# Rounded two-pass scores over stacked key halves, keys and queries single-buffered and projected last, latents' weights in one tile

## The reference, cut to what matters

```python
def fox_attend(q, k, v, cum_q, cum_k, pos_q, pos_k):
    s = jnp.einsum('bqhd,bkhd->bhqk', q, k).astype(jnp.float32) * (HEAD_DIM ** -0.5)
    decay = jnp.transpose(cum_q, (0, 2, 1))[..., :, None] - jnp.transpose(cum_k, (0, 2, 1))[..., None, :]
    visible = pos_k[None, :] <= pos_q[:, None]
    p = jax.nn.softmax(jnp.where(visible, s + decay, NEG_INF), axis=-1)
    return jnp.einsum('bhqk,bkhd->bqhd', p.astype(v.dtype), v)

def sb_attend(q, k, v, pos_q, pos_k):
    z = jnp.einsum('bqhd,bkhd->bhqk', q, k).astype(jnp.float32) * (HEAD_DIM ** -0.5)
    before = pos_k[None, :] < pos_q[:, None]
    log_beta = jnp.where(before, jax.nn.log_sigmoid(z), NEG_INF)
    log_rest = jnp.where(before, jax.nn.log_sigmoid(-z), 0.0)
    later = lax.cumsum(log_rest, axis=log_rest.ndim - 1, reverse=True) - log_rest
    a = jnp.exp(log_beta + later)
    return jnp.einsum('bhqk,bkhd->bqhd', a.astype(v.dtype), v)

# layer 1, mla_project
    z = h @ w_down                       # D_MODEL x (384 + 256 + 32)
    cq, ckv, kr = jnp.split(z, [Q_LORA, Q_LORA + KV_LORA], axis=-1)
```

## Time and profile before

| | before |
|---|---|
| median of 3 runs | 1449.56 us |
| profiled execution | 1455.13 us, span 1453.4 us |
| busy share PE / PEld / DVE / ACT / POOL | 83% / 57% / 45% / 27% / 17% |
| mean granted TensorE clock | 0.919 of full |
| first layer's eight pairs | 45.05 to 341.2 us of the span |
| latents of layer 1 | 722 to 791 us |

### The profile page before, as it was taken

The page is one execution under the profiler, slowest core; times in us unless marked ns, Lnnn a source line. Parts: engine busy times, 40 slices in busy tenths (PEclk is TensorE's granted clock), DMA queues, the critical chain, the costliest instruction groups (busy, mean ns, idle before and its releaser), DMA issues. The chain is left out here.

```text
span 1453.4 us, 23857 instructions
## 1 busy us (share of the span) xinstructions
PE 1203.3 (83%) x8148; PEld 833.9 (57%) x8148; DVE 655.4 (45%) x1819; ACT 391.2 (27%) x903; POOL 239.9 (17%) x366
## 2 busy tenths in 40 slices
PE   7999999987966997777497899999799499877760
PEld 5777777765854564344264676766587355444430
DVE  5455544446571542122362355555566445222227
ACT  4334444445111211011121244444521021111111
POOL 1222232220103232221110000000001222222113
PEclk9899999999977999999798999999899599989995
DMA  5222324206169999999620300000032999999965
GB/s 177 76 68 74 105 91 147 94 18 243 73 286 339 375 364 374 378 372 411 255 75 19 131 17 16 31 15 16 22 143 119 365 374 359 359 374 384 394 275 195
DMA packets 61407, 290.75 MB, mean 200 GB/s; under 512 B 12720, under 2 KB 23152, under 8 KB 44288
## 3 DMA queue, kind: packets, MB, share of 16 engines
q1 hardware_dynamic: 49440, 265.90, 49.5%
q0 software_dynamic: 10560, 18.90, 4.1%
q10 hardware_dynamic: 1312, 4.72, 0.8%
HBM read 275.91 MB, written 29.29 MB: 210 GB/s over the span
## 5 line engine op out<-in xcount | busy, mean ns | idle before, releaser
L1738 PE MATMUL psum<-w_gu,moe_xgT 128*64 128x256 f32 x1968 | 261.2, 410 | 71.1 <-DMA w_gu<-in_w_gate_up 56.1
L1738 PEld LDWEIGHTS psum<-w_gu,moe_xgT 128*64 128x64 f32 x1968 | 154.2, 146 | 162.3 <-issue 116.3
L199 PE MATMUL psum<-x_hi,ab_w_hi 128*128 128x288 f32 x384 | 126.6, 330 | 2.7 <-DVE ab_k_tok L877 1.6
L1811 DVE COPY moe_xgT<-psum 128x512 f32<-128x512 f32 x64 | 44.3, 692 | 166.0 <-PE psum L1728 165.1
L201 PE MATMUL psum<-x_hi,ab_w_lo 128*128 128x288 f32 x384 | 115.7, 301 | 0.0
L1685 POOL DMA_INDIRECT y_d<-mix,moe_slots x60 | 55.5, 926 | 364.0 <-DVE mix L1824 364.0
L200 PE MATMUL psum<-x_lo,ab_w_hi 128*128 128x288 f32 x384 | 115.6, 301 | 0.0
L1786 ACT ACTIVATE moe_silu<-psum 64x256 f32<-64x256 f32 x64 | 24.2, 378 | 338.9 <-PE psum L1738 293.8
L1755 PE MATMUL psum<-w_dn,moe_hidT 128*64 128x512 f32 x352 | 85.1, 604 | 2.2 <-issue 2.2
L1819 DVE COPY moe_hidT<-psum 128x128 f32<-128x128 f32 x64 | 18.7, 291 | 143.1 <-PE psum L1746 141.5
L199 PEld LDWEIGHTS psum<-x_hi,ab_w_hi 128*128 128x128 f32 x384 | 74.5, 194 | 9.5 <-issue 7.6
(11 more groups left out here) (305 smaller groups left out, 2124.0 us busy)
## 6 DMA issues: line engine op xcount, KB each, us to landing
w_gu<-in_w_gate_up SPq DMA_DIRECT2D x54, 2048.0 KB, 35.4
w_dn<-in_w_down SPq DMA_DIRECT2D x44, 1024.0 KB, 37.4
xT<-in_w_down SPq DMA_DIRECT2D x20, 1024.0 KB, 38.6
w_gu<-in_w_gate_up SPq DMA_DIRECT2D x10, 1536.0 KB, 40.5
w_gu<-in_w_out SPq DMA_DIRECT2D x4, 2048.0 KB, 7.9
combine_ys<-y_d SPq DMA_DIRECT2D x16, 512.0 KB, 8.5
xT<-in_w_gate_up SPq DMA_DIRECT2D x10, 512.0 KB, 41.8
xT<-cum_d SPq DMA_DIRECT2D x8, 544.0 KB, 6.6
```

The costliest lines, as they stand in the source:

```text
L199: nc.tensor.matmul(dst, r32(ah), r32(bh), start=first, stop=False)
L1738: last = nc.tensor.matmul(gu(s)[h * CB:(h + 1) * CB, 0:EH], xgT[:, s, j, :], gate_up_tile(k.w_gu[n], j)[:, h * EH:(h + 1) * EH], start=(j ...
L1811: nc.vector.tensor_copy(xgT[:, s, :, :].rearrange("p j q -> p (j q)"), xtr(s)).then_inc(xgT_ready, 1)
```

## The change

Scores of layer 0. The scaled queries and the keys are now split into a rounded half and a rest as the projections' operands are. A tile `k_both[h]` holds the keys' rounded half in the 64 partitions of the head and the rest in the other 64; `q_hi[h]` holds the rounded queries twice, once for each; `q_lo[h]` holds the queries' rest over the rounded keys and zeros over the others. A score is then two rounded passes, `q_hi` and `q_lo` over `k_both`, where before it was one f32 product; the product of the two rests is left out. All of these tiles are single; the past keys get a tile of their own (`k_past`) and are split into `k_both` at the start of each pair, on ScalarE at u = 0 and on VectorE at u = 1 (`split_past`).

Since queries and keys are single, pair p+1's may be written only when pair p's scores are all issued: the values are projected first and the queries and keys last (`AB_AFTER`, `AB_WEIGHTS`). Copies of q1 and k1 grow from one instruction on each engine (two on VectorE for k1) to four and two for q1, two and three for k1. SP loads the past keys of the next pair only after VectorE has split those of this one.

Latents. The tile `mix` is lengthened so that all 672 columns of the latents' weights lie side by side in it; the product now streams two ranges, of 512 and 160 columns. The last 32 columns are loaded into it in pieces of 128 bytes for each of eight rows of a partition, where before they were 1024 bytes in one piece.

```diff
-        self.w_latent = self.mix[:, :, :].rearrange("p t d -> p (t d)").rearrange("p (j n) -> p j n", j=J)
-        self.w_rope = sb("w_rope", [P, J, ROPE])
+        self.w_latent = mix_room[:].rearrange("p (j n) -> p j n", j=J)
...
-AB_AFTER = {"q0": -1, "q1": 0, "k0": 2, "k1": 3, "kt": 4, "v0": 5, "v1": 7, "vt": 8}
+AB_AFTER = {"v0": -1, "v1": 0, "vt": 2, "q0": 3, "q1": 5, "k0": 6, "k1": 7, "kt": 8}
+AB_WEIGHTS = (2, 0, 1)
+AB_ROOM = (1, 0, 0)
+PAST_AT = T
...
-            qh = [[sb(f"q{a}{h}", [P, T]) for h in range(2)] for a in range(2)]
-            kT = [sb(f"kT{a}", [P, KEYS]) for a in range(2)]
-            kh = [[kT[a], kT[a]] for a in range(2)]
+            q_hi = [sb(f"q_hi{h}", [P, T]) for h in range(2)]
+            q_lo = [sb(f"q_lo{h}", [P, T]) for h in range(2)]
+            k_both = [sb(f"k_both{h}", [P, KEYS]) for h in range(2)]
+            k_past = sb("k_past", [P, PAST])
+            kT = sb("kT", [P, T])
...
+                        hold(sp, passed, (s["o_ready"], NT * (p - 1)), (s["kp_lo"], p))
+                    sp.dma_start(k_past[:], row(k.k_past, p)).then_inc(s["kp_in"], 16)
...
-                        banks_free(p, (0, 1, 3)[n], (s[f"lo{n}"], p + 1))
+                        banks_free(p, (2, 3, 0)[n], (s[f"lo{n}"], p + 1))
...
+                        hold(pe, passed, (s["scored"], n - u + used + 1), *([(s["kp_lo"], p + 1)] if u == UNITS - 2 and not mla else []))
+                    at_t = slice(t * P, t * P + rows)
+                    if mla:
+                        q, key = qh[par][h][0:QW, at_t], kh[par][h][0:QW, lo:lo + width]
+                        last = nc.tensor.matmul(slot(u)[0:rows, 0:min(width, BANK)], q, key[:, 0:min(width, BANK)], start=True, stop=True)
+                        if width > BANK:
+                            last = nc.tensor.matmul(slot(u)[0:rows, BANK:width], q, key[:, BANK:width], start=True, stop=True)
+                    else:
+
+                        pieces = [(0, width, 0)] if t < 4 else [(0, PAST, PAST_AT), (PAST, width, SEQ)]
+                        for q, first in ((q_hi[h], True), (q_lo[h], False)):
+                            for a, b, at in pieces:
+                                last = nc.tensor.matmul(slot(u)[0:rows, a:b], r32(q[:, at_t]), r32(k_both[h][:, at:at + b - a]),
+                                                        start=first, stop=not first)
...
-            copied = list(MLA_AFTER) if mla else ["q1", "k1", "kt", "v1", "vt"]
+            copied = list(MLA_AFTER) if mla else ["v1", "vt", "q1", "k1", "kt"]
...
                 if u == 1 and not last(1):
-                    split(p + 1, 1 - par, 2)
-                if u == 4 and not last(2):
+                    split(p + 1, 1 - par, 1)
+                if u == 6 and not last(2):
+                    split(p + 2, par, 2)
+                if u == 8 and not last(2):
                     split(p + 2, par, 0)
-                if u == 8 and not last(2):
-                    split(p + 2, par, 1)
...
+                        def q1():
+                            copy(by_half(r32(q_hi[0][0:HD, :])), halves[0:HD], HD ** -0.5).then_inc(s["q_hi_done"], 1)
+                            copy(by_half(r32(q_hi[1][HD:P, :])), halves[HD:P], HD ** -0.5).then_inc(s["q_hi_done"], 1)
+                            hold(act, passed, (s["q_hi_done"], 2 * p + 2))
+                            copy(r32(q_hi[0][HD:P, :]), q_hi[0][0:HD, :])
+                            return copy(r32(q_hi[1][0:HD, :]), q_hi[1][HD:P, :])
+
+                        def k1():
+                            copy(by_half(r32(k_both[0][0:HD, 0:T])), halves[0:HD]).then_inc(s["k_hi_done"], 1)
+                            return copy(by_half(r32(k_both[1][HD:P, 0:T])), halves[HD:P])
...
+                def split_past(p):
+                    hold(act, passed, (s["kp_in"], 16 * (p + 1)), (s["scores_ready"], UNITS * p))
+                    copy(r32(k_both[0][0:HD, PAST_AT:]), k_past[0:HD, :])
+                    copy(r32(k_both[1][HD:P, PAST_AT:]), k_past[HD:P, :]).then_inc(s["kp_hi"], 1)
...
+                        if u == 0 and not mla:
+                            split_past(p)
...
+                        def q1():
+                            hold(dve, passed, (s["q_hi_done"], 2 * p + 1))
+                            v.scalar_tensor_tensor(by_half(r32(q_lo[0][0:HD, :])), halves[0:HD], HD ** -0.5, by_half(q_hi[0][0:HD, :]), ALU.mult, ALU.subtract)
+                            hold(dve, passed, (s["q_hi_done"], 2 * p + 2))
+                            return v.scalar_tensor_tensor(by_half(r32(q_lo[1][HD:P, :])), halves[HD:P], HD ** -0.5, by_half(q_hi[1][HD:P, :]), ALU.mult, ALU.subtract)
+
                         def k1():
-                            v.tensor_copy(kT[par][:, HT:SEQ], halves[:, 1, 0:SEQ - HT])
-                            return v.tensor_copy(kT[par][:, NEW_AT:KEYS], halves[:, 1, SEQ - HT:HT])
+                            hold(dve, passed, (s["k_hi_done"], p + 1))
+                            v.tensor_tensor(by_half(r32(k_both[0][HD:P, 0:T])), halves[0:HD], by_half(k_both[0][0:HD, 0:T]), ALU.subtract)
+                            hold(dve, passed, (s["proj_act"], n))
+                            v.tensor_tensor(by_half(r32(k_both[1][0:HD, 0:T])), halves[HD:P], by_half(k_both[1][HD:P, 0:T]), ALU.subtract)
+                            return v.tensor_copy(by_half(kT[:]), halves)
...
+                def split_past(p):
+                    hold(dve, passed, (s["kp_hi"], p + 1))
+                    split_lo(nc, k_both[0][HD:P, PAST_AT:], k_past[0:HD, :], k_both[0][0:HD, PAST_AT:])
+                    split_lo(nc, k_both[1][0:HD, PAST_AT:], k_past[HD:P, :], k_both[1][HD:P, PAST_AT:]).then_inc(s["kp_lo"], 1)
...
+                        if u == 1 and not mla:
+                            split_past(p)
...
-            for lo, hi, w in ((0, BANK, k.w_latent[:, :, 0:BANK]), (BANK, DOWN - ROPE, k.w_latent[:, :, BANK:]), (DOWN - ROPE, DOWN, k.w_rope)):
+            for lo, hi in ((0, BANK), (BANK, DOWN)):
                 for j in range(J):
-                    last = nc.tensor.matmul(z(t)[0:ROWS[t], lo:hi], k.xT[:, j, t * P:t * P + ROWS[t]], w[:, j, :],
+                    last = nc.tensor.matmul(z(t)[0:ROWS[t], lo:hi], k.xT[:, j, t * P:t * P + ROWS[t]], k.w_latent[:, j, lo:hi],
```

70 lines of the change are left out of this document (29 added, 41 removed).

## The result

The changed kernel takes 1516.52 us (median of 4 runs, 1512.27 to 1525.05) against 1449.9 of the kernel before, run beside it: a ratio of 1.0465, 95% interval 1.0417 to 1.0513. The forecast was slower, 1483; the time lies above its range (1456 to 1501). The profiled execution took 1518.34 us (span 1516.6), 63.2 more than that of before.

The account below looks back on a forecast made before the run. TensorE was taken to set the pace. Seven pairs 30, last pair 0.5, before the first 3, latents -5.7 and clock 6 summed to +33.8 us on 1449.56, giving 1483, range 1456 to 1501.

Parts of the forecast that it names:

- The clock: TensorE at 1.2 GHz behind long waits: four more slow stretches over seven pairs, +6 us (0 to 21).
- narrow pieces: Scores of 128 and 64 columns, with no rounded row to judge by: taken as +0.5 us a pair.
- latents: Merged 160-column product in the latents' weights, in place of 128 and 32: -5.7 us together.
- The waits: TensorE idle in each projecting pair: 7.85 us added, 1.4 of present gaps gone, +6.5 a pair.
- Places 1 to 4: Idle before unit 2's transposes 1.7, unit 3's 0.7, keys' projection 2.5, keys' transposes 2.85 us, each pair.
- Score work: Two rounded passes in place of one f32 product, units of 256 to 512 columns: -2.55 us a pair.
- Before the first pair: Query and key copies there lie uncovered, in longer chains than now: +3 us (0 to 4).
- last pair: Pair without projections, 22.7 us: added ScalarE and VectorE copies against shorter scores, +0.5 us (-1 to +2).
- A: Rival: waits don't form, score work decides, 1422 us; milder form 1433; 12 in 100.
- B: Rival: places 1 and 2 stay covered, clock holds, 3 and 4 stand: +10, 1460 us; 12 in 100.
- C: Rival: a rounded score pass is no faster than an f32 product: 1510 to 1550 us; 3 in 100.
- D: Rival: later transfers of keys and weights come late for their splits: 1490 to 1500 us; 3 in 100.

Follow-up runs that it names:

- e7: Kernel before, old order, each score as two rounded passes, queries' remainder and past keys left out (not the full result): 1436.0 us, ratio 0.9897.
- e3: Changed kernel with queries' and keys' banks copied out once into kT and the stacked halves made from SBUF: 1485.0 us, ratio 1.0260.
- e6: Kernel before with TensorE made to wait twice a pair, before the keys' projection and transposes, for a 128 KB transfer: 1474.1 us, ratio 1.0148.
- e9: Kernel before with TensorE waiting before the keys' projection and transposes for transfers in 64-byte pieces: 1492.2 us, ratio 1.0306.
- e13: Kernel before with TensorE waiting before the keys' projection and transposes for transfers in 32-byte pieces: 1521.4 us, ratio 1.0479.
- e15: Kernel before with two TensorE waits a pair for transfers in 64-byte pieces, before the values' projection and the values' transposes: 1498.0 us, ratio 1.0334.
- e14: As e3, with rounded products filling waits before the keys' projection and transposes and the transposes of units 2, 3 and 9: 1473.8 us, ratio 1.0170.

## Why the prediction was wrong

The direction and four of its places were right, and two terms were mis-sized.

1. **The clock, the step that failed.** The forecast counted "four more such stretches over the seven pairs: +6", from above 21. Four stretches of 3.3 us are 13 us; there were some 100 more at half clock, and they cost 39 us (changed kernel against e7), 33 more than counted. The price of a us at half clock was not too low (1.5 us for 3.3, or 0.45, against 0.38 measured); the amount was. The forecast's change fell 33 us short in the medians and 29 between the two profiled executions; the other misses (waits +5, narrow pieces -3, latents and the rest -5) nearly cancel. It took the count from a pair with a single wait of 1.9 us and added per long wait. But in e3, with 87 us slow, all waits but two (2.7 and 4.1 us) are at most 1.63, and slow time grows more than in proportion to idle time (e6, e9, e13). The step should have asked how much of the whole pair TensorE would idle: 3.3 us of 38 before, about 10 of 50 after. Why so much of the pair then fell to half clock is open beyond that (below). The Trainium skill, "TensorE: Matmul & The Clock Gate", "HAM oscillation — how this bites in real kernels", says that waits between bursts of products bring the throttle back each time. The granted clock of e9, e13 and e15 agrees, e6's does not yet.
2. **The waits.** Forecast 45.5 us over seven pairs, measured 50.8 in the attention. Places 1 to 4 were within 0.15 us each. The fifth, before the queries' projection, up to 1.6 us and 9.1 in all, was missed: the forecast put that projection behind unit 3's wait as something covered. Against it the wait at the pair's end, which the forecast kept at 1.89, shrank to at most 1.2 (11.4 us before, 5.2 after).
3. **Score work.** Forecast -20 us and 3.5 for the narrow pieces; e7 shows -19.9 of busy time, so the narrow pieces cost about nothing. In the changed kernel's last pair at 2.4 GHz:

```profile
391.25 0.34 PE L646 MATMUL psum<-ab_k_both,ab_q_hi 128*128 128x128 f32 x1
391.42 0.28 PE L646 MATMUL psum<-ab_k_both,ab_q_lo 128*128 128x128 f32 x1
391.54 0.27 PE L646 MATMUL psum<-ab_k_both,ab_q_hi 128*128 128x128 f32 x1
391.65 0.28 PE L646 MATMUL psum<-ab_k_both,ab_q_lo 128*128 128x128 f32 x1
391.76 0.34 PE L646 MATMUL psum<-ab_k_both,ab_q_hi 128*128 128x256 f32 x1
391.93 0.28 PE L646 MATMUL psum<-ab_k_both,ab_q_lo 128*128 128x256 f32 x1
392.06 0.28 PE L646 MATMUL psum<-ab_k_both,ab_q_hi 128*128 128x256 f32 x1
392.17 0.28 PE L646 MATMUL psum<-ab_k_both,ab_q_lo 128*128 128x256 f32 x1
```

Behind the first a 128-column pass leaves after 0.11 to 0.12 us, start to start; so two of them cost about what the two records of one f32 product did. A weight load stands before each pass, and these start 0.11 us apart too; whether they set the step was not tested:

```profile
391.48 0.19 PEld L646 LDWEIGHTS psum<-ab_k_both,ab_q_hi 128*128 128x128 f32 x1
391.59 0.19 PEld L646 LDWEIGHTS psum<-ab_k_both,ab_q_lo 128*128 128x128 f32 x1
```

The Trainium skill, "TensorE: Matmul & The Clock Gate", "Back-to-back issue gap", gives about 81 ns for a 128-column product in a stream of products with weight loads, and 56 ns for an isolated one. No step here is under 0.11 us, so for these 4-byte operands the trace disagrees with both. The wider passes came out as forecast: 0.23 us from a pass of 512 columns to the next product (212.56 to 212.79 in the fourth pair).
4. **Before the first pair** +3.4 against +3; **last pair** 22.0 us, by the same landmarks 21.3 before (forecast +0.5); **latents** -4.3 timed against -5.7; the 128-byte pieces cost nothing visible: the load lands 11.6 us after its issue, 10.9 before, and TensorE starts with a wait of 1.11 us for ScalarE in both traces.
5. **Rivals.** A and B needed covered waits; none was. C is refuted by e7. D did not come: no wait of TensorE in the attention is ended by a transfer.

What stays open: at about equal idle time (52 to 57 us) e9 has 33 us slow, e15 53, e3 87. From e9 to e15 the waits' place and the length of one changed together; what makes the step to e3 was not isolated. The changed order has more, shorter waits, and e14 shows that filling them works, but no run spread e3's waits without filling them.
